# A 1 MB weight load dealt as 119 and 9 partitions, in a mixture-of-experts layer on one core

## The chip, the cores and the metric

The kernel runs on one core of a Trainium2 chip. Its time is that of the device, in microseconds, from the start to the end of one execution; of several executions the median counts. The core has TensorE (PE in the rows, with PEld for its weight loads), VectorE (DVE), ScalarE (ACT), GpSimd (POOL) and SyncE (SP), and 16 DMA engines that all its transfers share.

## The reference, cut to what matters

One decoder layer on 256 tokens of 1024 columns, in float32. First a mixing part (retention and block attention), then a mixture of 32 experts, of which each token takes four:

```
h2 = rms_norm(x, norm2_w)                       # 256 x 1024
logits = h2 @ w_router + b_router               # 32 experts
gate, chosen = softmax over the top 4 logits
for each expert e, for its tokens:
    u = h2[tokens] @ w1[e] + b1[e]              # 1024 -> 2048
    a = clamped_swiglu(u)                       # -> 1024
    x[tokens] += gate * (a @ w2[e] + b2[e])     # 1024 -> 1024
out = rms_norm(x, final_norm_w)
```

An expert has 8 MB of `w1` (the first layer) and 4 MB of `w2` (the second). All 32 are read once: 384 MB.

## The kernel before

The expert part takes 64 token slots per expert. The tokens of an expert are gathered by a matmul with a 0/1 matrix, turned, multiplied with `w1` (`up`, its matmuls at L1444), put through the SwiGLU, turned again, multiplied with `w2` (`down_part`, L1466), and added back by another 0/1 matmul (`combine`, L1415).

The weights stream through `ring`, an area of 24 slots of 1 MB, used as 12 pairs of 2 MB. A step of the loop over experts has six chunks of 2 MB: chunks 0 to 3 are the `w1` of expert j, chunks 4 and 5 the two halves of `w2` of expert j - 1. So step j does the up projection of expert j and the down projection of expert j - 1. Chunk `(j, k)` goes to pair `pair_of(j, k)`. Steps 6 to 17 of the source form the body of a loop that runs twice, in which `w1` chunks are loaded two at a time (4 MB, L430); the last steps stand behind it. Step 30 is written out as `LAST - 1`, step 31 as `LAST`, and step `E` = 32 holds only the last down projection.

SyncE issues every weight load, in the order of use, into one queue. Before each it waits until PE has used what stood in the pair (`chunk_used`). `load` (L432 to L445) picks the form: most chunks are one DMA of 128 partitions by 16 KB (L443 for `w1`, L445 for `w2`). The chunks in `END_HALVES`, the last ones of the kernel, are two DMAs of 128 partitions by 8 KB (L440, L441), and the very last chunk is three DMAs (L437), so that PE can begin with a part. The DMAs of a pair count up its semaphore `pair_full[d]` by 16.

PE's `down` (L1471) waits for `pair_full` of its chunk, then does 16 matmuls over the whole chunk: columns 0 to 2047 of the pair (slots `2d`) with the activations `c` = 0, 1, and columns 2048 to 4095 with `c` = 2, 3.

Bias rows are loaded once, near 111 us, by three DMAs of 32 partitions by 4 KB (L456, L457). `final_norm_w` is loaded last (L536).

Of the kernel before, what the change touches and what calls it, by code (L numbers as in the profile page):

```python
# [23 lines left out]
P = 128  # L24
SEQ = 256
T = SEQ // P
D = 1024
# [21 lines left out]
W1_CHUNKS = C // 2  # L49
# [7 lines left out]
LAST = E - 1  # L57
BIAS_STEP, RESID_STEP = 4, 5
LAST_PARTS = [(0, 2), (2, 3), (3, 4)]
END_HALVES = [(LAST, W1_CHUNKS), (LAST, W1_CHUNKS + 1), (E, 0)]  # L60
assert PEEL + ITERS * UNROLL + 2 == E and TURNS * PAIRS == UNROLL * STEP_CHUNKS
SENTINEL = 3.0e38
# [33 lines left out]
def local_expert(i, j):  # L96

    return i * UNROLL + j
# [7 lines left out]
def down_chunk(j, k):  # L106

    return k if j == E else k - W1_CHUNKS

def place_in_stream(j, k):

    return k if j == 0 else j * STEP_CHUNKS - W2_CHUNKS + k

def pair_of(j, k):

    return place_in_stream(j, k) % PAIRS
# [7 lines left out]
def pair_count(r, i, j, k):  # L126

    g = place_in_stream(j, k)
    per_round = len(range(g % PAIRS, ROUND_CHUNKS - 1, PAIRS))
    if g % PAIRS in {pair_of(j, k) for j in (PEEL, PEEL + 1) for k in range(1, W1_CHUNKS, 2)}:  # L130
        in_loop = ITERS * TURNS
        return 16 * (r * (per_round - in_loop) + (g // PAIRS + 1) - (in_loop if j >= PEEL + UNROLL else 0))
    return 16 * (r * per_round + i * TURNS + (g // PAIRS + 1))

def layer_kernel(nc, x, norm1_w, w_in, ret_norm_w, w_out, norm2_w, w_router, b_router,
# [6 lines left out]
    w2_v = w2.rearrange("l e (q p s) n -> (l e) q p (s n)", p=P, s=4)  # L143

    ctx = ExitStack()
    with ctx:
# [3 lines left out]
        def sem(name):  # L150
            return ctx.enter_context(nc.semaphore(name))
# [4 lines left out]
        def bank(b, n=1):  # L156
            return PS[:, b * BANK:(b + n) * BANK]
# [103 lines left out]
        head_full = [sem(f"head_full{s}") for s in range(HEAD_CHUNKS)]  # L261
        last_in = [sem(f"last_in{k}") for k in range(len(LAST_PARTS))]
        half_in = [sem(f"half_in{k}") for k in range(len(END_HALVES))]
        pair_full = [sem(f"pair_full{d}") for d in range(PAIRS)]
        chunk_used = sem("chunk_used")
        early_used = sem("early_used")
        early_in = [sem(f"early_in{k}") for k in range(len(EARLY))]
# [126 lines left out]
        def _(sp):  # L394
# [14 lines left out]
            for j, pair in enumerate(WOUT_ORDER):  # L409
                s = WIN_CHUNKS + j  # L410
                dst = ring[:, s, :].rearrange("p (c n) -> p c n", c=2)
# [10 lines left out]
            def w1_half(e, k):  # L422

                return w1_v[e, k // 2, :, (k % 2) * 2 * SLOT_COLS:(k % 2 + 1) * 2 * SLOT_COLS]
# [7 lines left out]
            def load(r, i, j, k):  # L432
                e, d = local_expert(i, j), pair_of(j, k)
                dst = ring[:, 2 * d:2 * d + 2, :].rearrange("p a n -> p (a n)")
                if j == E and k == W2_CHUNKS - 1:
                    for part, (a, b) in enumerate(LAST_PARTS):
                        sp.dma_start(dst[:, a * D:b * D], w2_v[e - 1, k, :, a * D:b * D]).then_inc(last_in[part], 16)  # L437
                elif (j, k) in END_HALVES:
                    src = w2_v[e - 1, down_chunk(j, k), :, :]
                    sp.dma_start(dst[:, 0:2 * D], src[:, 0:2 * D]).then_inc(half_in[END_HALVES.index((j, k))], 16)  # L440
                    sp.dma_start(dst[:, 2 * D:], src[:, 2 * D:]).then_inc(pair_full[d], 16)  # L441
                elif j < E and k < W1_CHUNKS:
                    sp.dma_start(dst, w1_half(e, k)).then_inc(pair_full[d], 16)  # L443
                else:
                    sp.dma_start(dst, w2_v[e - 1, down_chunk(j, k), :, :]).then_inc(pair_full[d], 16)  # L445

            for g in FIRST_ORDER:
                if g == 10:
                    sp.wait_ge(decayed_ready, RET_HEADS)
                    sp.wait_ge(chunk_used, WIN_CHUNKS)  # L450
                elif g == 11:
                    sp.wait_ge(probT_ready, MOBA_HEADS)
                    sp.wait_ge(pv_done, 4)
                    sp.wait_ge(ret_done, RET_HEADS)
                    for v in range(2):
                        sp.dma_start(b1_sb[v * E:(v + 1) * E, :], b1[0, :, v * F:(v + 1) * F]).then_inc(late_in, 16)  # L456
                    sp.dma_start(b2_sb, b2[0, :, :]).then_inc(late_in, 16)  # L457
                    sp.wait_ge(gated, T)
                elif g == 8:
                    sp.wait_ge(retT_done, 2)  # L460
                elif g == 9:
                    sp.wait_ge(retT_done, 2)
                    sp.wait_ge(chunk_used, HEAD_CHUNKS - 2)
                else:
                    sp.wait_ge(chunk_used, min(2 * g + 2, HEAD_CHUNKS))
                if g == MOVED:
                    d = pair_of(0, g)
                    sp.dma_start(ring[:, 2 * d, :], w1_half(0, g)[:, 0:SLOT_COLS]).then_inc(pair_full[d], 16)
                    sp.dma_start(ring[:, 2 * d + 1, :], w2_v[1, 1, :, SLOT_COLS:]).then_inc(ahead_in, 16)
                elif g < W1_CHUNKS:  # L470
                    load(0, 0, 0, g)
                else:
                    load(0, 0, 1 + (g - W1_CHUNKS) // STEP_CHUNKS, (g - W1_CHUNKS) % STEP_CHUNKS)
# [619 lines left out]
        def _(pe):  # L1093
# [325 lines left out]
            def wait_early(r, g):  # L1419

                if isinstance(r, int) and g - PAIRS in EARLY:
                    pe.wait_ge(early_in[EARLY.index(g - PAIRS)], 16)
                    if g - PAIRS in QUARTERS:
                        pe.wait_ge(early_v0_in[QUARTERS.index(g - PAIRS)], 16)
# [35 lines left out]
            def down_part(j, k, c0, c1, aT_n, out):  # L1460

                d, h = pair_of(j, k), down_chunk(j, k)
                for c in range(c0, c1):
                    for half in range(2):
                        cols = (c % 2) * D + half * BANK
                        last = mm(out[64 * half:64 * half + 64, :], aT_n[:, c, 64 * h:64 * h + 64],  # L1466
                                  ring[:, 2 * d + c // 2, cols:cols + BANK],
                                  start=(h == 0 and c == 0), stop=(h == 1 and c == 3))
                return last

            def down(r, i, j, k):  # L1471

                pe.wait_ge(pair_full[pair_of(j, k)], pair_count(r, i, j, k))
                g = place_in_stream(j, k)
                wait_early(r, g)
                if isinstance(r, int) and g == AHEAD:
                    pe.wait_ge(ahead_in, 16)
                aT_n, out = (aT_last, bank(1)) if j == E else (aT, bank(5))
                down_part(j, k, 0, 4, aT_n, out).then_inc(chunk_used, 1)

            def down_first(r, j, k):

                pe.wait_ge(half_in[END_HALVES.index((j, k))], 16 * (r + 1))
                aT_n, out = (aT_last, bank(1)) if j == E else (aT, bank(5))
                down_part(j, k, 0, 2, aT_n, out)

            def down_rest(r, i, j, k):

                pe.wait_ge(pair_full[pair_of(j, k)], pair_count(r, i, j, k))
                aT_n, out = (aT_last, bank(1)) if j == E else (aT, bank(5))  # L1490
                down_part(j, k, 2, 4, aT_n, out).then_inc(chunk_used, 1)
# [21 lines left out]
            def end_step(r, i):  # L1513
# [5 lines left out]
                down_rest(r, i, E, 0)  # L1519
                for part, (c0, c1) in enumerate(LAST_PARTS):  # L1520
                    pe.wait_ge(last_in[part], 16 * (r + 1))
# [7 lines left out]
            def expert_pe(r, i, j):  # L1529
# [16 lines left out]
                if j > 0:  # L1546
                    pe.wait_ge(actT_ready, n)
                    for k in range(W1_CHUNKS, STEP_CHUNKS):
                        down(r, i, j, k)
# [96 lines left out]
```

## Time and profile before

| | |
|---|---|
| median of 3 runs | 1052.78 us (1052.59 to 1054.54) |
| the profiled execution | 1053.78 us |
| its span, first to last instruction | 1052.0 us |
| PE busy | 1028.2 us, 98% |
| VectorE, ScalarE busy | 221.5, 117.5 us |
| queue q1, share of the 16 DMA engines | 96.3% |
| moved | 424.62 MB, mean 404 GB/s |

A share of 1 in a column "DMA share" means that all 16 DMA engines are busy in that stretch; packets that overlap at their ends can bring it a little over 1. PE's matmuls are pipelined and their ends modelled, so that small waits don't show as idle time. "Issue to landing" of a DMA runs from its issue on SyncE to the last count of its semaphore, and includes the time in the queue behind earlier ones.

### The profile page before, as it was taken

How to read it: one execution, taken by the hardware profiler on the slowest of the kernel's cores; microseconds unless marked ns; L12 is line 12 of the kernel's file. 1: busy time of each engine (PE TensorE's matmuls, PEld its weight loads, DVE VectorE, ACT ScalarE, POOL GpSimd, SP SyncE). 2: the span in 40 equal slices, each digit the busy share in tenths (PEclk: the TensorE clock that was granted, in tenths of full speed). 3: DMA queues.
4: the chain of work that ended last, by engine and by line, in shares of the span. 5: the costliest groups of instructions: out<-in, count | busy, mean ns of one | idle time of the engine just before them, and what ended most of it. 6: DMA issues, size and time to landing. Idle time of an engine off the chain costs nothing.

```text
span 1052.0 us, 11246 instructions
## 1 busy us (share of the span) xinstructions
PE 1028.2 (98%) x4918; PEld 415.7 (40%) x4918; DVE 221.5 (21%) x585; ACT 117.5 (11%) x223; POOL 0.2 (0%) x4
## 2 busy tenths in 40 slices
PE   9999999999999999999999999999999999998996
PEld 8888543333333333333333333333333333323332
DVE  2173442111111111111111111111111111111111
ACT  2131130000000000000000000000000000000002
POOL 0000000000000000000000000000000000000000
PEclk9999999999999999999999999999999999999999
DMA  9982999999999999999999999999999999999995
GB/s 320 369 363 80 351 371 386 410 429 434 420 424 400 437 427 430 434 428 429 427 425 431 434 429 430 430 430 433 424 427 428 433 432 427 433 428 426 428 422 224
DMA packets 39126, 424.62 MB, mean 404 GB/s; under 512 B 3512, under 2 KB 16320, under 8 KB 19744
## 3 DMA queue, kind: packets, MB, share of 16 engines
q1 hardware_dynamic: 38768, 423.51, 96.3%
q8 instruction: 41, 0.67, 0.3%
q10 hardware_dynamic: 304, 0.33, 0.1%
q14 instruction: 13, 0.11, 0.0%
HBM read 422.78 MB, written 1.05 MB: 403 GB/s over the span
## 4 chain that ended last, share of the span: by engine, by line
PE 92%; DMA 5%; another core or an unknown queue 1%; DVE 1%; issue 0%; ACT 0%; SPq 0%; DVEq 0%; ACTq 0%
PE PS L1444 41%; PE PS L1466 20%; PE PS L1122 8%; PE PS L1415 5%; DMA ring<-in_w 5%; PE PS L1398 5%; PE PS L1303 3%; PE PS L1259 3%; PE PS L1497 2%; PE PS L1407 2%; PE PS L1390 1%; DMA ring<-in_w_in 1%; PE PS L1571 0%; PE PS L1585 0%; PE PS L1192 0%
## 5 line engine op out<-in xcount | busy, mean ns | idle before, releaser
L1444 PE MATMUL PS<-ring,work 128*64 128x512 f32 x2040 | 448.7, 596 | 12.0 <-DMA ring<-in_w 10.7
L1444 PEld LDWEIGHTS PS<-ring,work 128*64 128x64 f32 x2040 | 143.9, 137 | 291.9 <-issue 273.4
L1466 PE MATMUL PS<-ring,work 128*64 128x512 f32 x1024 | 227.4, 595 | 0.1
L1466 PEld LDWEIGHTS PS<-ring,work 128*64 128x64 f32 x1024 | 70.6, 137 | 153.8 <-issue 151.1
L1015 DVE TENSOR_SCALAR work<-PS 128x512 f32<-128x512 f32 x32 | 22.1, 692 | 401.1 <-PE PS L1444 401.1
L1122 PE MATMUL PS<-ring 128*128 128x256 f32 x384 | 85.4, 380 | 0.3 <-DMA ring<-in_w_in 0.3
L644 ACT ACTIVATE work<-work 128x512 f32<-128x512 f32 x32 | 20.2, 630 | 535.3 <-DVE work L1015 535.3
L1122 PEld LDWEIGHTS PS<-ring 128*128 128x128 f32 x384 | 72.0, 190 | 10.8 <-DMA ring<-in_w_in 0.7
L983 DVE TENSOR_TENSOR work<-PS,n2w 128x512 f32<-128x512 f32 x30 | 20.8, 692 | 228.3 <-PE PS L1407 228.3
L1415 PE MATMUL PS<-late,work 64*128 64x512 f32 x248 | 61.9, 616 | 0.0
L1398 PE MATMUL PS<-resid,work 128*64 128x512 f32 x248 | 58.5, 592 | 0.0
L661 ACT ACTIVATE late<-PS 128x512 f32<-128x512 f32 x30 | 17.9, 597 | 209.6 <-PE PS L1466 209.6
L1303 PE MATMUL PS<-work 32*64 32x512 f32 x256 | 34.8, 613 | 0.0
L1398 PEld LDWEIGHTS PS<-resid,work 128*64 128x64 f32 x248 | 17.8, 137 | 35.4 <-issue 35.4
L991 DVE COPY work<-PS 128x256 f32<-128x256 f32 x31 | 13.2, 425 | 85.9 <-PE PS L1390 85.9
L1415 PEld LDWEIGHTS PS<-late,work 64*128 64x128 f32 x248 | 21.3, 186 | 19.4 <-issue 15.8
L1407 PEld LDWEIGHTS PS<-cst,work 128*128 128x128 f32 x124 | 17.3, 209 | 25.4 <-issue 24.3
L1497 PE MATMUL PS<-cst,work 128*128 128x128 f32 x128 | 23.9, 309 | 0.5
L1407 PE MATMUL PS<-cst,work 128*128 128x128 f32 x124 | 23.2, 310 | 0.1
L1019 DVE SCALAR_TENSOR_TENSOR work<-work 128x512 f32<-128x512 f32 x32 | 22.2, 692 | 3.3
L1022 DVE TENSOR_TENSOR work<-work 128x512 f32<-128x512 f32 x32 | 22.1, 692 | 1.1
L664 ACT ACTIVATE work<-PS 128x512 f32<-128x512 f32 x31 | 18.5, 597 | 30.8 <-PE PS L1497 30.8
(173 smaller groups left out, 370.2 us busy)
## 6 DMA issues: line engine op xcount, KB each, us to landing
ring<-in_w SPq DMA_DIRECT2D x48, 4096.0 KB, 34.9
ring<-in_w SPq DMA_DIRECT2D x85, 2048.0 KB, 27.1
ring<-in_w SPq DMA_DIRECT2D x18, 1024.0 KB, 9.7
ring<-in_w_in SPq DMA_DIRECT2D x11, 1024.0 KB, 11.9
ring<-in_w_out SPq DMA_DIRECT2D x4, 1024.0 KB, 12.1
ring<-in_w SPq DMA_DIRECT2D x6, 512.0 KB, 6.9
ring<-in_w_in SPq DMA_DIRECT2D x2, 512.0 KB, 6.3
ring<-in_consts SPq DMA_DIRECT2D x1, 800.0 KB, 11.2
```

The source lines that it names most:

```text
L1015: nc.vector.tensor_scalar(g_sb, bank(0), LIMIT, None, ALU.min).then_inc(gate_ready, 1)
L1019: nc.vector.scalar_tensor_tensor(a_sb, a_sb, 1.0, g_sb, ALU.add, ALU.mult).then_inc(glin_ready, 1)
L1022: nc.vector.tensor_tensor(a_sb, a_sb, s_sb, ALU.mult).then_inc(act_ready, 1)
L1122: last = mm(bank(4 + j % 2)[:, t * WIN_COLS:(t + 1) * WIN_COLS], hT[:, t, c, :], w[:, c, :], start=(c == 0), stop=(c == C - 1))
L1259: return mm(bank(2 + 4 * t + j), mixT(c)[:, t * P:(t + 1) * P], w[:, c % 2, j * BANK:(j + 1) * BANK], start=(c == 4), stop=(c == 3))
L1303: last = mm(bank(v)[64 * half:64 * half + 64, :], sel[v * E:(v + 1) * E, :], b1_sb[v * E:(v + 1) * E, half * BANK:(half + 1) * BANK], star ...
L1398: last = mm(bank(4)[64 * half:64 * half + 64, :], pick[:, t, :], resid[:, t, half_cols(half)], start=(t == 0), stop=(t == T - 1))
L1407: last = nc.tensor.transpose(bank(4)[:, c * P:(c + 1) * P], gx_v[:, c, :], ident)
L1415: last = mm(bank(2 + 4 * t + half), put[rows, t * P:(t + 1) * P], y[rows, :], start=start, stop=False, skip_group_check=True)
L1444: last = mm(bank(v)[64 * half:64 * half + 64, :], gh[:, c, :], w[:, v * F + half * BANK:v * F + (half + 1) * BANK], start=False, stop=(c = ...
L1466: last = mm(out[64 * half:64 * half + 64, :], aT_n[:, c, 64 * h:64 * h + 64], ring[:, 2 * d + c // 2, cols:cols + BANK], start=(h == 0 and ...
L1497: last = nc.tensor.transpose(out[:, c * P:(c + 1) * P], a_v[:, c, :], ident)
```

## The change

Chunk 4 of step 30, the first half of expert 29's second layer, is loaded as three DMAs instead of one: columns 0 to 2047 in two DMAs, of the rows 0 to 118 and 119 to 127, and columns 2048 to 4095 in one of 128 rows. The first two count up a semaphore of their own, `split_in`, for which PE's `down` waits beside `pair_full`.

```diff
+SPLIT, SPLIT_ROWS = (LAST - 1, W1_CHUNKS), 119
...
+        split_in = sem("split_in")
...
                     sp.dma_start(dst[:, 0:2 * D], src[:, 0:2 * D]).then_inc(half_in[END_HALVES.index((j, k))], 16)
                     sp.dma_start(dst[:, 2 * D:], src[:, 2 * D:]).then_inc(pair_full[d], 16)
+                elif (j, k) == SPLIT:
+                    src = w2_v[e - 1, down_chunk(j, k), :, :]
+                    for rows in (slice(0, SPLIT_ROWS), slice(SPLIT_ROWS, P)):
+                        sp.dma_start(dst[rows, 0:2 * D], src[rows, 0:2 * D]).then_inc(split_in, 16)
+                    sp.dma_start(dst[:, 2 * D:], src[:, 2 * D:]).then_inc(pair_full[d], 16)
                 elif j < E and k < W1_CHUNKS:
...
                 if isinstance(r, int) and g == AHEAD:
                     pe.wait_ge(ahead_in, 16)
+                if (j, k) == SPLIT:
+                    pe.wait_ge(split_in, 32 * (r + 1))
```

## Rows read from the trace of the kernel before

**Rows 1.** The page: busy time by engine, and the DMA queues.
```profile
PE 1028.2 (98%) x4918; PEld 415.7 (40%) x4918; DVE 221.5 (21%) x585; ACT 117.5 (11%) x223; POOL 0.2 (0%) x4
q1 hardware_dynamic: 38768, 423.51, 96.3%
```

**Rows 2.** Stages; columns: stretch, length, busy by engine, PE's clock, DMA share, GB/s.
```profile
300.00:500.00 200.00, 199.88 (x943) 69.66 (x940) 33.88 (x77) 16.95 (x28) 0.00 (x0) 1.00 1.00 426
700.00:900.00 200.00, 194.60 (x922) 66.76 (x918) 33.91 (x77) 16.95 (x28) 0.00 (x0) 1.00 1.01 430
```

**Rows 3.** The chain that ended last, steady stage: start, length, what (one of three).
```profile
899.71 1.64 another core or an unknown queue
```

**Rows 4.** The same chain, the last experts.
```profile
958.39 2.49 another core or an unknown queue
...
960.93 8.78 PE PS L1444 x32
...
983.19 13.88 PE PS L1444 x64
...
999.81 7.02 PE PS L1466 x32
...
1024.44 3.43 PE PS L1466 x16
...
1028.77 3.58 PE PS L1466 x16
1032.36 0.13 issue
...
1035.49 5.49 PE PS L1466 x24
```

**Rows 5.** SyncE's DMA issues in order of time: start, length, line, count.
```profile
111.14 0.80 SPq L456 DMA_DIRECT2D work<-in_b  x2
...
944.04 6.46 SPq L445 DMA_DIRECT2D ring<-in_w  x2
...
1002.24 16.14 SPq L437 DMA_DIRECT2D ring<-in_w  x3
```

**Rows 6.** One line's DMAs: first that of L445 at 944.04 alone.
```profile
DMA to landing us min/median/max: 51.5/51.5/51.5
L440 SPq DMA_DIRECT2D ring<-in_w x3: 4241/4245/4599, 976.2 to 993.7; - x3
DMA to landing us min/median/max: 38.7/42.3/46.3
L437 SPq DMA_DIRECT2D ring<-in_w x3: 1137/2712/12207, 1002.2 to 1015.7; - x3
DMA to landing us min/median/max: 24.1/35.0/35.1
```

**Rows 7.** The end of the stream, in stretches; columns as in rows 2.
```profile
1033.00:1034.00 1.00, 1.00 (x8) 0.29 (x4) 0.00 (x0) 0.98 (x2) 0.00 (x0) 1.00 1.05 414
1034.00:1035.00 1.00, 1.00 (x6) 0.30 (x4) 0.00 (x0) 0.50 (x2) 0.00 (x0) 1.00 0.71 295
1035.00:1037.00 2.00, 2.00 (x12) 0.48 (x8) 0.00 (x0) 0.00 (x0) 0.00 (x0) 1.00 0.55 227
...
1039.00:1040.00 1.00, 1.00 (x8) 0.32 (x6) 0.00 (x0) 0.00 (x0) 0.00 (x0) 1.00 0.31 119
1040.00:1041.00 1.00, 1.00 (x8) 0.19 (x4) 0.00 (x0) 0.00 (x0) 0.00 (x0) 1.00 0.10 41
```

**Rows 8.** Stretches around the three loads of 32 partitions.
```profile
113.00:115.00 2.00, 2.00 (x6) 0.95 (x5) 1.62 (x14) 0.21 (x1) 0.00 (x0) 1.00 1.01 434
118.00:118.50 0.50, 0.50 (x2) 0.19 (x1) 0.47 (x2) 0.00 (x0) 0.00 (x0) 1.00 0.99 221
118.50:119.50 1.00, 1.00 (x4) 0.40 (x3) 0.54 (x1) 0.00 (x0) 0.00 (x0) 1.00 1.06 279
```

**Rows 9.** PE's clock after its long stop.
```profile
961.80:965.10 3.30, 3.30 (x10) 0.98 (x8) 0.00 (x0) 0.00 (x0) 0.00 (x0) 0.50 0.99 422
```

## The prediction before the run

> **What bounds the kernel now.** I read the page first, then the stages, then the tail piece by piece. The page says two things at once: PE is busy for 98% of the span, and the queue of the loads, q1, keeps the 16 DMA engines busy for 96.3% of it [rows 1]. The stages tell them apart. From 300 to 900 us the DMA share is 1.00 to 1.01 at 426 to 430 GB/s, and nothing else is full [rows 2]. An expert is 12 MB of weights, and the chain repeats the same pattern: PE works through 32 + 32 + 8 + 8 + 32 + ... matmuls and then stands for 1.6 us (three times from 870 to 931, one row shown) [rows 3]. So up to the last three experts the weight stream is the bound, and PE has some 1.6 us to spare per expert.
>
> At the end this turns. The last long stop is 2.49 us at 958.39. From 983.19 on the chain is PE alone [rows 4]: two up projections of 13.88 us (the second, at 1010.56, is like the one shown), without a stop, and down projections behind them. PE and the stream are then nearly equal. How near is read from pieces of the same kind. Sixteen down matmuls take 3.43 us at 1024.44 but 3.58 us at 1028.77; 0.13 us is "issue"; and the last 24 take 5.49 us, where 24 at the rate of the undisturbed 32 in 7.02 us would take 5.27. That is 0.15 + 0.13 + 0.22 = 0.5 us of waiting for weights in the last 58 us, and no more. The last megabyte, in three parts, is issued from 1002.2 to 1015.7, and its parts land 24.1 to 35.1 us later, the very last at 1015.7 + 24.1 = 1039.8 [rows 5, 6], and PE ends the down projection that needs it at 1040.98. So in the tail a landing that is earlier can give at most 0.5 us, and one that is later is paid in full.
>
> **Where the changed DMA sits.** It is the first half of the 2 MB load that SP issues at 944.04; that lands 51.5 us later, at 995.5 [rows 5, 6]. PE wants it at 999.81 [rows 4], so 4.3 us of cover. It isn't the chunk itself that matters then, but what the 16 engines have behind it: 2 MB + 4 x 2 MB + the 1 MB and 0.5 MB pieces, all queued on the same engines without a gap up to 1039.8.
>
> **What it adds.** (a) One DMA becomes three: two more issues at 0.33 us on SP. SP issues the later ones 24 to 50 us ahead of their landing [rows 6], and where its issue takes 4 to 16 us [rows 5] it waits for room in queues that are full, so that this is hidden; were it not, it would be under 1 us. Each more DMA has a completion entry of its own on each engine: the 1 MB pieces of L440 and L441 land from 976.2 + 46.3 = 1022.5 to 993.7 + 38.7 = 1032.4, four pieces in 9.9 us or 2.48 us each [rows 6], while 1.05 MB at the 430 GB/s of the larger loads [rows 2] are 2.44 us; the 0.04 us are for the entry, twice 0.08. (b) PE waits for one more semaphore before the first half of a down projection. Behind it stand on PE the 32 down matmuls, the turning of rows and activations, the combine and the last up projection, and VectorE and ScalarE wait for those; with 4.3 us of cover it costs nothing unless the piece is over 4.3 us late.
>
> **(c) How the rows are dealt.** This is the term that decides. 128 rows are 8 rows for each of 16 engines. 119 = 7 x 17 can't be dealt evenly to 16; even shares exist on seven engines (or one) only, and 9 rows are one each on nine. I take it that the shares are even: 17 rows on each of seven engines, then one more row on these and on two others. The trace of before has no load with such a number, so the bounds are uneven dealing (7 or 8 rows each, no effect) and this.
> The Trainium skill ("DMA: Bandwidth & Descriptors", section "Why a DMA increments its semaphore by 16 and not by 1") states that the engine count is the largest number up to 16 that divides the slowest dimension, and that the lowest-numbered engines are taken; by that it is seven and nine. No row of this profile shows it.
>
> An 8 KB row at 430 GB/s / 16 = 26.9 GB/s is 0.305 us. The seven have 18 rows to do instead of 8: 10 x 0.305 = +3.05 us on them, and the other nine 7 or 8 rows less, -2.1 to -2.4 us.
>
> **(d) Are the seven the ones that are ahead?** The 16 engines do not end together. The DMA share is 1.05 at 1033, 0.71 in 1034 to 1035, then 0.55, then 0.31 in 1039 to 1040 and 0.10 in the last microsecond before 1041 [rows 7]. 9 of 16 is 0.56: seven engines run dry at about 1034.3 (0.71 is 0.56 + 0.34 of the other 0.44), all of them before 1035, and nine work on until 1039.7 on average (1039 + 0.41/0.56) and 1041.0 at the latest. So seven are 6.7 us ahead on average and at least 6.0. Every load waits for its slowest engine. If the seven that get more are those seven, +3.05 us is inside their lead, and the nine end earlier. If they are others, all +3.05 us is paid. The counts agree and no row gives the engines' numbers; I take "the same seven" at 4 to 1.
>
> **(e) Do they write at full speed?** In before each engine always takes the same rows of a 128-row load. There is one place with other shapes: three bias loads of 32 rows each, issued from 111.14 on [rows 5]. While they pass, the engines are as busy as ever (share 0.99 to 1.06) and move 221 and 279 GB/s, against 434 ahead of them [rows 8]. Engines that write rows other than those of the usual deal slow one another, down to 221/434 = 0.51 of the rate. So for the 18 rows the bounds are 18 x 0.305 = 5.5 us (full speed) and 18 x 0.61 = 11.0 us (half). Against 8 x 0.305 = 2.44 us in before that is +3.05 or +8.5 us. For the nine others, half speed on what they meet takes back the 2.1 to 2.4 us. I take half speed for the most unlucky of the seven, because rows 8 are the nearest thing here, and the load ends with its slowest engine.
> The Trainium skill ("SBUF — State Buffer", section "Door 1: The DMA port swizzle") gives a port to each group of 8 partitions and 27.2 GB/s to a port; with that, seven engines that reach all 119 partitions write through the ports of the nine as well. The trace agrees as far as rows 8 go; in those rows half of the ports would carry it all.
>
> **The sum.** Seven leading engines, the slowest at half rate: +8.5 - 6.0 (least lead) = +2.5, and entries 0.1, and some 0.2 because a PE that now stops does not stop at the best places: +2.8 us. Nothing in the tail hides it: PE's own slack is there already used up, the last landing moves, and the ends of the down projection, of the last combine and of the norm move with it. The profiled execution took 1053.78 us for a span of 1052.0, which would become 1056.6 and 1054.8; it was 1.0 above the median of 1052.78, so the median becomes 1055.6.
>
> **The rivals.**
> R1, not slower: the seven are the leaders and write at full speed. Then the nine decide, end 2.1 us earlier, and PE is the bound: of 2.1 us only the 0.5 us of waiting can be had, less 0.1: 1052.4. For it: the lead of 6.0 to 6.7 is twice the 3.05 us. Against it: rows 8. It holds as long as the seven lose less than 6.0 us, that is while their rate in the 18 rows stays over 0.65 of full.
> R2: the seven are not the leaders. At full speed +3.1, 1055.9; at half speed +8.5 and up to 1061.3. For it: nothing ties the numbers of the engines to their lead. Against: seven and nine on both sides.
> R3: the change doesn't do that. Rows are dealt as evenly as can be on 16 engines, nothing but 0.1 us of entries: 1052.9.
> R4, on top of the forecast or of R2: PE's clock. PE stood for 2.49 us from 958.39 on [rows 4], and in the stretch behind that the granted clock was 0.50, which is 1.2 GHz [rows 9]; the 32 matmuls in it took 8.78 instead of 7.09 us: 1.7 us. Stops of 1.6 us, one per expert, did not do it [rows 3]. If the new waits come in one piece like that one, the end is at 1057.3.
>
> **How the numbers follow.** Forecast (leaders, about half rate, 1.5 to 5 us lost) 0.38, with R4's share in it; R1 0.25; R2 0.15; R3 0.12; the seven only a little slower than their lead allows, 0 to 1.5 us lost, 0.10. A measurement tells about 0.2%, 2.1 us. Slower by more: most of the forecast (0.34), all of R2 (0.15) and a little of the rest with R4 (0.06): 0.55. Within: 0.43. Faster by more: only were PE not the bound, 0.02. The range of 8 in 10 goes from R1 (1052.1) to half of R2 (1059.0).
>
> **What would show it.** If the even deal is right: a DMA share that differs in the tail from 0.56 for 4 to 5 us. In the forecast all 16 engines end within some 2 us of one another, the share stays near 1 up to some 1038, and the last landing is at about 1042.6; the chain has stops for weights of 2 to 3 us in all after 1002. In R1 the share stays near 1 up to 1037 and then falls at once, and the pieces of the last down projections are down to 3.43 us for 16. In R2 the engines that are last stand alone: a share of 0.44 or less for up to 9 us. In R3 rows 7 come back as they are. The stream itself must slow just once, around 985 to 996, if writing is what costs: GB/s under 400 at a share of 1. If GB/s stays at 430 there, step (e) is wrong; if the last landing is over 1043.5, the leads were read wrongly.

## The result: 13 us slower, and the trace after

Timed side by side on one chip, the changed kernel takes 1067.93 us (median of 4 runs, 1066.18 to 1070.96), the kernel before 1053.58 (4 runs, 1052.59 to 1054.54). The ratio is 1.0127, 95% interval 1.0104 to 1.0151: about +13.4 us (the medians by themselves are 14.35 apart). I had forecast 1055.6, which is +2.8, with a range up to 1059.0. The profiled execution took 1066.18 us for a span of 1064.4.

Page of the kernel after, totals by engine (busy us, share, instructions). PE is busy for 5.8 us more than before with the same work:

```profile
span 1064.4 us, 11248 instructions
PE 1034.0 (97%) x4918; PEld 416.8 (39%) x4918; DVE 221.4 (21%) x585; ACT 117.6 (11%) x223; POOL 0.2 (0%) x4
```

Where it goes is seen in the stages. Kernel after, busy time by stretch; the last three columns are PE's granted clock, DMA share and GB/s, as in [rows 2]:

```profile
980.00:984.00 4.00, 4.00 (x22) 1.51 (x22) 1.47 (x6) 0.00 (x0) 0.00 (x0) 1.00 1.07 412
984.00:988.00 4.00, 4.00 (x22) 1.35 (x20) 0.00 (x0) 0.00 (x0) 0.00 (x0) 1.00 1.01 246
988.00:992.00 4.00, 2.94 (x14) 0.72 (x10) 0.00 (x0) 0.00 (x0) 0.00 (x0) 1.00 0.95 205
992.00:996.00 4.00, 0.62 (x2) 0.30 (x4) 0.00 (x0) 0.00 (x0) 0.00 (x0) 0.66 1.05 225
996.00:1000.00 4.00, 4.00 (x12) 1.19 (x10) 0.00 (x0) 0.00 (x0) 0.00 (x0) 0.50 1.02 227
1000.00:1004.00 4.00, 4.00 (x22) 0.91 (x18) 2.45 (x4) 1.05 (x2) 0.00 (x0) 0.99 1.01 246
...
1006.00:1010.00 4.00, 1.87 (x6) 0.72 (x8) 0.00 (x0) 0.00 (x0) 0.00 (x0) 0.62 1.02 436
```

For 20 us the 16 engines are as busy as ever and move about half. It isn't only the changed half: in 20 us they would have moved 8.6 MB, and in these 20 us they moved some 4.6. The loads ahead of the half and behind it slow down with it. To size it, one stretch that holds all of it, of the kernel before and then of the kernel after:

```profile
976.00:1024.00 48.00, 47.96 (x230) 17.05 (x227) 6.47 (x15) 3.62 (x6) 0.00 (x0) 1.00 1.01 426
```

```profile
976.00:1024.00 48.00, 39.49 (x164) 13.84 (x162) 6.46 (x15) 3.62 (x6) 0.00 (x0) 0.86 1.01 339
```

The share is the same 1.01. I call **stream lost** what is missing in the bytes, in us: 48 x (1 - 339/426) = 9.8 us.

The landings, lines of DMA issues of the kernel after (first the last `w1` chunk of step 30, which the change doesn't touch; then the third DMA of the split chunk; then the very last parts), and the counterpart of the first in the kernel before:

```profile
L450 SPq DMA_DIRECT2D ring<-in_w x1: 328/328/328, 937.4 to 937.4; - x1
DMA to landing us min/median/max: 57.9/57.9/57.9
...
L448 SPq DMA_DIRECT2D ring<-in_w x1: 3597/3597/3597, 957.4 to 957.4; - x1
DMA to landing us min/median/max: 50.6/50.6/50.6
...
L439 SPq DMA_DIRECT2D ring<-in_w x3: 3933/4240/4243, 1017.2 to 1025.8; - x3
DMA to landing us min/median/max: 26.5/29.6/32.6
```

```profile
L443 SPq DMA_DIRECT2D ring<-in_w x1: 328/328/328, 937.7 to 937.7; - x1
DMA to landing us min/median/max: 52.9/52.9/52.9
```

The `w1` chunk ahead of the split lands at 937.4 + 57.9 = 995.3 instead of 990.6 (+4.7). The split chunk lands at 957.4 + 50.6 = 1008.0 instead of 995.5 [rows 6] (+12.5). The very last part lands at 1025.8 + 26.5 = 1052.3 instead of 1039.8 (+12.5), and PE ends the last down projection at 1053.53 instead of 1040.98. So nothing is added or given back after 1008: the place costs 12.5 us and the tail hands it on. (This execution was 0.8 us ahead of the one of before until then: the second `w1` chunk of step 30 landed at 980.03 instead of 980.81. Counted from there the loss is 13.3, which agrees with the 13.4 of the ratio.)

PE's queue of the kernel after, start and length, with the idle time ahead in brackets, shows the two stops:

```profile
995.38 5.98 PE L1451 MATMUL PS<-ring,work 128*64 128x512 f32 x16 [4.44 <-DMA ring<-in_w]
...
1008.13 4.54 PE L1473 MATMUL PS<-ring,work 128*64 128x512 f32 x10 [4.04 <-DMA ring<-in_w]
```

The end of the stream, kernel after, columns as above; it answers to [rows 7]:

```profile
1036.00:1040.00 4.00, 4.00 (x21) 1.37 (x18) 2.67 (x4) 0.63 (x1) 0.00 (x0) 1.00 1.01 417
1040.00:1042.00 2.00, 2.00 (x14) 0.85 (x12) 0.42 (x1) 0.60 (x1) 0.00 (x0) 1.00 0.96 391
1042.00:1044.00 2.00, 1.92 (x12) 0.48 (x8) 0.00 (x0) 0.00 (x0) 0.00 (x0) 1.00 0.79 320
1044.00:1046.00 2.00, 1.40 (x9) 0.43 (x7) 0.00 (x0) 1.45 (x2) 0.00 (x0) 1.00 0.82 330
1046.00:1050.00 4.00, 4.00 (x20) 1.06 (x18) 0.00 (x0) 0.64 (x2) 0.00 (x0) 1.00 0.28 116
1050.00:1053.00 3.00, 3.00 (x16) 0.93 (x16) 0.00 (x0) 0.00 (x0) 0.00 (x0) 1.00 0.11 44
```

Before, nine engines worked together almost to the end. Now 0.28 of 16 is 4 to 5 engines and 0.11 is two: the engines end farther apart. Capacity left unused until the last landing: 2 x 0.04 + 2 x 0.21 + 2 x 0.18 + 4 x 0.72 + 2.3 x 0.89 = 5.8 us, against 0.29 + 4 x 0.45 + 0.8 x 0.69 = 2.6 before [rows 7]. These 3.2 us and the 9.8 of the stream make 13.0; the landing moved by 12.5.

**Which engines had the 119 rows.** The semaphores' counts in the trace of after give the ends of each engine's part (us). First the `w1` chunk ahead, then both pieces of the split half, then the third DMA:

```
w1 ahead   983.7 983.7 983.7 983.8 984.0 984.1 984.9 | 986.8 | 991.7 991.8 992.3 992.5 993.0 993.1 994.3 995.3
119 + 9    (944.2 957.6) 984.5 984.8 993.4 993.4 994.0 994.3 994.4 994.8 994.9 995.5 998.3 998.9 1004.3 1004.6 1005.4 1005.8
third DMA  988.2 988.5 988.8 996.6 996.7 997.1 997.3 997.7 997.8 998.7 998.7 999.3 1000.0 1003.2 1007.0 1008.0
```

The two in brackets come right after the issues. Behind them are 16 = 7 + 9 counts, one for each engine that did a part.
The Trainium skill ("DMA: Bandwidth & Descriptors", section "Why a DMA increments its semaphore by 16 and not by 1") says that the issuer counts at once for the engines that a DMA doesn't use, and gives seven and nine; this line agrees.

In the first line seven engines lead by some 8 us (in the second `w1` chunk of step 30, where nothing is slowed yet, by 4 to 6: 973.9 to 974.6 against 978.3 to 980.0). Had they had the 17 rows, no count of the split could stand at 984.5 and 984.8, and no third-DMA part at 988.2 to 988.8. Three leaders had none of the 17. The rest follows from 8 rows at some 0.6 us behind each end. Six ends of the third DMA, 996.6 to 997.8, stand 4.7 to 4.9 us behind the first six laggards of the first line (991.7 to 993.1), so that these had none either. So the seven that did were four leaders, the one in the middle and two laggards. Four leaders in the seven, three outside: a lead has nothing to do with the dealing.

The last two ends of each line are those two laggards: from 994.3 and 995.3 to 1004.6 and 1005.8, 18 rows in 10.3 and 10.5 us. That is 0.57 to 0.58 us a row, near the half rate that I had taken (0.61).

### The profile page after: what moved, and what is told of

Read it like the earlier page. It is cut to its first block, busy times and chain, and to the rows that moved or that the text cites. A ratio compares the mean times of both kernels' runs of the same rounds, so it can differ in the third digit from the quotient of the medians.

```text
span 1064.4 us, 11248 instructions
## 1 busy us (share of the span) xinstructions
PE 1034.0 (97%) x4918; PEld 416.8 (39%) x4918; DVE 221.4 (21%) x585; ACT 117.6 (11%) x223; POOL 0.2 (0%) x4
## 3 DMA queue, kind: packets, MB, share of 16 engines
HBM read 422.78 MB, written 1.05 MB: 398 GB/s over the span
## 4 chain that ended last, share of the span: by engine, by line
PE 83%; DMA 13%; SPq 2%; DVE 1%; another core or an unknown queue 1%; issue 0%; ACT 0%; DVEq 0%; ACTq 0%
PE PS L1451 36%; PE PS L1473 17%; DMA ring<-in_w 13%; PE PS L1129 8%; PE PS L1422 5%; PE PS L1405 4%; PE PS L1266 3%; PE PS L1310 2%; PE PS L1506 2%; PE PS L1414 2%; SPq L443 2%; PE PS L1397 1%; DMA ring<-in_w_in 1%; PE PS L1580 0%; PE PS L1594 0%
## 5 line engine op out<-in xcount | busy, mean ns | idle before, releaser
L1451 PE MATMUL PS<-ring,work 128*64 128x512 f32 x2040 | 451.3, 599 | 14.4 <-DMA ring<-in_w 13.3
L998 DVE COPY work<-PS 128x256 f32<-128x256 f32 x31 | 13.2, 425 | 86.0 <-PE PS L1397 86.0
```

What stands on the lines that cost most here:

```text
L1451: last = mm(bank(v)[64 * half:64 * half + 64, :], gh[:, c, :], w[:, v * F + half * BANK:v * F + (half + 1) * BANK], start=False, stop=(c = ...
```

## The experiments

Each edit is shown against the changed kernel; all times are against the kernel before on the same chip. The column "us" is the ratio less 1, times the median of before; the medians themselves differ from that by up to 1.3 us. "Lost" is the stream lost as above, from the one row 976 to 1024 of each trace (before: 426 GB/s). "Ahead" and "split" are by how much the `w1` chunk ahead and the split chunk land later than before. They are counted from the landing of the second `w1` chunk of step 30, from which before needs 9.78 and 14.69 us.

| cut of the half | GB/s | lost | ahead | split | ratio (95%) | us |
|---|---|---|---|---|---|---|
| by columns, 1904 and 144 | 424 | 0.2 | 0.0 | 0.1 | 1.0008 (0.9986 to 1.003) | +0.8 |
| own rows only | 425 | 0.1 | 0.0 | 0.1 | 1.0004 (0.9983 to 1.0025) | +0.4 |
| other rows only | 379 | 5.3 | 3.8 | 6.1 | 1.0041 (1.0025 to 1.0057) | +4.3 |
| 112 and 16, of 1024 columns | 401 | 2.8 | 2.8 | 3.5 | 1.0014 (0.9997 to 1.0031) | +1.5 |
| 64 and 64 | 371 | 6.2 | 4.9 | 6.7 | 1.0057 (1.0033 to 1.0081) | +6.0 |
| 112 and 16 | 365 | 6.9 | 5.6 | 7.5 | 1.0069 (1.0052 to 1.0087) | +7.3 |
| 120 and 8 | 373 | 6.0 | 4.4 | 7.1 | 1.0072 (1.0054 to 1.0091) | +7.6 |
| 117 and 11, first run | 366 | 6.8 | 4.8 | 7.5 | 1.0053 (1.0036 to 1.007) | +5.6 |
| 117 and 11, second run | 366 | 6.8 | 4.8 | 7.6 | 1.0072 (1.004 to 1.0104) | +7.6 |
| 115 and 13 | 354 | 8.1 | 6.2 | 9.0 | 1.0092 (1.0068 to 1.0116) | +9.7 |
| 114 and 14 | 352 | 8.3 | 6.0 | 13.2 | 1.0118 (1.0086 to 1.015) | +12.5 |
| 119 and 9 (the change) | 339 | 9.8 | 5.5 | 13.3 | 1.0127 (1.0104 to 1.0151) | +13.4 |
| 119 and 9, again | 336 | 10.1 | 6.2 | 13.8 | 1.0136 (1.0108 to 1.0165) | +14.4 |

### Is it the rows, or one DMA more?

The half in two DMAs of all 128 rows, with nearly the same bytes in each.

```diff
-                    for rows in (slice(0, SPLIT_ROWS), slice(SPLIT_ROWS, P)):
-                        sp.dma_start(dst[rows, 0:2 * D], src[rows, 0:2 * D]).then_inc(split_in, 16)
+                    for cols in (slice(0, 1904), slice(1904, 2 * D)):
+                        sp.dma_start(dst[:, cols], src[:, cols]).then_inc(split_in, 16)
```

> The half is cut by columns instead of rows: three DMAs as in the changed kernel, all of 128 partitions (1904, 144 and 2048 columns). Theory M (rows that reach partitions other than those of the usual deal slow the whole stream) and theory I (ten more rows on each of seven engines): both expect the time of before, within 0.5 us, and a stream at 420 to 430 GB/s all through 984 to 1004 us. Theory N (it is the number of DMAs, their entries, or the wait added on PE): expects a good part of the 12 us of the change here too.

1.0008: nothing. Busy time by stretch of this kernel, columns as above:

```profile
984.00:988.00 4.00, 4.00 (x22) 1.31 (x20) 0.00 (x0) 0.00 (x0) 0.00 (x0) 1.00 1.01 418
...
992.00:996.00 4.00, 4.00 (x22) 1.29 (x18) 0.94 (x2) 0.21 (x1) 0.00 (x0) 1.00 1.04 440
```

The three issues, the wait and the entries cost nothing that can be told: the interval of the times reaches from -1.5 to +3.2 us, but the split chunk lands only 0.1 us later. All that follows is the cut by rows.

### Is it the uneven deal?

112 and 16 rows are even on 16 engines, 120 and 8 on 15 and 8.

```diff
-SPLIT, SPLIT_ROWS = (LAST - 1, W1_CHUNKS), 119
+SPLIT, SPLIT_ROWS = (LAST - 1, W1_CHUNKS), 112
```

> The rows are cut as 112 and 16: both numbers divide evenly over 16 engines (7 and 1 rows each), so no engine gets more than before, but nearly every engine writes other partitions than in a DMA of 128. Theory M: most of the loss of the change stays, plus 6 to 12 us over before, and the stream runs at 200 to 300 GB/s at a DMA share near 1 for 10 to 20 us. Theory I: the time of before, within 0.5 us, since no engine has more to do.

> Rows cut as 120 and 8: 15 engines with 8 rows, then 8 engines with one more; the most loaded engine has 9 rows instead of 8, 0.3 us more. Theory I: plus 0.3 us or less. Theory M: plus 6 to 12 us, as with 112 and 16.

+7.3 and +7.6 us: more than half of the loss is there with 8 rows, or at most 9, for each engine. Kernel with 112 and 16, busy time by stretch:

```profile
984.00:988.00 4.00, 4.00 (x22) 1.41 (x21) 1.48 (x6) 0.00 (x0) 0.00 (x0) 1.00 1.07 227
988.00:992.00 4.00, 4.00 (x22) 1.43 (x20) 0.00 (x0) 0.00 (x0) 0.00 (x0) 1.00 0.94 287
992.00:996.00 4.00, 3.03 (x16) 0.72 (x10) 0.00 (x0) 0.00 (x0) 0.00 (x0) 1.00 1.04 233
996.00:1000.00 4.00, 2.72 (x8) 0.88 (x10) 0.00 (x0) 0.00 (x0) 0.00 (x0) 0.65 1.02 264
1000.00:1004.00 4.00, 4.00 (x20) 1.12 (x16) 1.29 (x2) 0.63 (x1) 0.00 (x0) 0.92 0.95 391
```

The same full share with 227 to 287 GB/s, for 16 us instead of 20. The uneven deal is what the change has on top of this, some 6 to 7 us.

### The same engines, bytes and count, on own or on other rows

Eight DMAs of 8 rows each, one row for each of eight engines. One kernel loads rows 0 to 63 so, in sets that leave each row to the engine that has it in a 128-row load; the other loads rows 64 to 127 with the same engines. The other 64 rows of the half aren't loaded in either, so that both leave part of the weights out.

```diff
-                    for rows in (slice(0, SPLIT_ROWS), slice(SPLIT_ROWS, P)):
+                    for first in (0, 1, 2, 3, 32, 33, 34, 35):
+                        rows = slice(0 + first, 0 + first + 29, 4)      # the other kernel: 64 + first
                         sp.dma_start(dst[rows, 0:2 * D], src[rows, 0:2 * D]).then_inc(split_in, 16)
...
-                    pe.wait_ge(split_in, 32 * (r + 1))
+                    pe.wait_ge(split_in, 128 * (r + 1))
```

> Instead of the two row pieces, eight DMAs of 8 rows by 8 KB: rows 0 to 63 in steps of four (0, 4, ... 28; 1, 5, ... 29; and so on; then 32 to 63). Rows 64 to 127 of the half are not loaded, so the output is not the reference's. An even deal is one row for each of eight engines. If in a DMA of 128 rows the first eight engines have rows 4e to 4e+3 and 32+4e to 35+4e, every row here is written by the engine that usually writes it. Theory M (it counts whether rows go to their usual engine): time of before or up to 1.3 us less, since eight engines move 0.5 MB less and the last may be among them; the stream never under 380 GB/s. Theory S (it is small or unevenly dealt DMAs that cost): plus 5 us or more, here and with rows 64 to 127 alike.

> The same eight DMAs, on rows 64 to 127; rows 0 to 63 of the half are not loaded, so the output is not the reference's. Same count, bytes and engines as its twin, but every row is one that another engine usually writes. Theory M: 0.5 MB on foreign rows, half of the 1 MB that cost 7.3 us with 112 and 16: plus 2.5 to 5 us over the twin, with the stream at 200 to 300 GB/s for 5 to 10 us. Theory S: within 0.5 us of the twin.

1.0004 and 1.0041; the intervals (to 1.0025, from 1.0025) only touch, and the median of the second is 5.6 us over that of the first. The traces leave less doubt. Own rows:

```profile
988.00:992.00 4.00, 4.00 (x22) 1.43 (x20) 0.00 (x0) 0.00 (x0) 0.00 (x0) 1.00 1.01 424
992.00:996.00 4.00, 4.00 (x22) 1.29 (x19) 0.92 (x2) 0.20 (x1) 0.00 (x0) 1.00 1.05 446
996.00:1000.00 4.00, 4.00 (x24) 1.08 (x22) 1.75 (x3) 1.03 (x2) 0.00 (x0) 1.00 0.98 418
```

Other rows (this execution was some 5 us late before step 30 had begun, so that its stretch stands later):

```profile
988.00:992.00 4.00, 4.00 (x22) 1.38 (x20) 0.00 (x0) 0.00 (x0) 0.00 (x0) 1.00 1.03 272
992.00:996.00 4.00, 4.00 (x20) 1.15 (x16) 0.00 (x0) 0.00 (x0) 0.00 (x0) 1.00 0.98 248
996.00:1000.00 4.00, 0.80 (x4) 0.29 (x4) 0.00 (x0) 0.00 (x0) 0.00 (x0) 0.81 1.05 295
```

This is the pair that settles the mechanism. Small DMAs, partial row counts and eight of 16 engines cost nothing; rows that another engine writes in the loads around cost the whole stream 5.3 us for 0.5 MB.
The Trainium skill ("DMA: Bandwidth & Descriptors", section "The descriptor swizzle") says which: engine e of 0 to 7 writes rows 4e to 4e + 3 and 32 + 4e to 32 + 4e + 3, and 8 to 15 the same from row 64 on. The two kernels were cut by that, and they agree.

The packets in the traces show the same one by one. With own rows the 16 KB packets of the ordinary loads take 611 to 627 ns each from 984 to 994 us, and the 8 KB packets 309 to 326. With other rows, from 990 to 994, the ordinary ones take 1039 to 1251 ns and the 8 KB ones 615 on average. In the changed kernel, from 988 to 996, the averages are 1206 and 612. Both sides of a collision run at half rate. What the pair doesn't tell is whether they collide where the rows are read or where they are written, since a row has the same number in `w2` and in the ring.

### How many engines share, and how few

64 and 64 rows, and 127 and 1.

```diff
-SPLIT, SPLIT_ROWS = (LAST - 1, W1_CHUNKS), 119
+SPLIT, SPLIT_ROWS = (LAST - 1, W1_CHUNKS), 64       # the other kernel: 127
```

 If it is the number of engines on the same rows' places that counts, two engines then share each of eight places in either DMA: plus 2.4 us at least (1 MB at half rate), and up to 7. Theory I (uneven deal alone): nothing.

> Rows cut as 127 and 1: an even deal exists on one engine only, which then has 128 rows instead of 8, 120 x 0.305 = 36.6 us more. Theory I: plus 36.6 us less the lead of that engine (0 to 6.8 us), so 30 to 37 us over before; the other 15 stay at their full rate, the stream at about 15/16 of 430 GB/s until they run dry. Theory M: one engine that visits all partitions also slows itself, row by row to half rate or less where it meets another: plus 40 to 75 us. If the deal is not even (uneven on 16 engines), plus nothing by I.

64 and 64 cost 6.0 us (3.5 to 8.5), over the 3 to 4.5 of a cost by rows and inside the 2.4 to 7 of its rival; the interval excludes neither. But the stream lost is 6.2 us against 6.9 with 112 and 16, so that the cost hardly fell. 127 and 1 cost 48.9 us (ratio 1.0463, 1.0434 to 1.0493), inside the 40 to 75 of theory M and over the 30 to 37 of theory I: one engine has all 128 rows. SyncE's queue and the busy time by stretch of that kernel:

```profile
947.02 55.38 SPq L447 DMA_DIRECT2D ring<-in_w  x2
1002.44 1.15 SPq L448 DMA_DIRECT2D ring<-in_w  x1
```

```profile
984.00:988.00 4.00, 4.00 (x22) 1.39 (x20) 1.48 (x6) 0.00 (x0) 0.00 (x0) 1.00 0.84 356
988.00:992.00 4.00, 4.00 (x22) 1.31 (x20) 0.00 (x0) 0.00 (x0) 0.00 (x0) 1.00 0.46 195
992.00:996.00 4.00, 4.00 (x20) 1.29 (x18) 0.00 (x0) 0.00 (x0) 0.00 (x0) 1.00 0.08 31
996.00:1000.00 4.00, 4.00 (x22) 1.29 (x18) 1.18 (x2) 0.46 (x1) 0.00 (x0) 1.00 0.06 27
```

Two things are read here. SyncE's two issues take 55 us, during which it can't issue the next load, and the other 15 engines run dry. And the one engine, alone, moves 27 GB/s, the full rate of one engine (430/16 = 26.9), though most of its rows are other engines' rows. So a foreign row isn't slow in itself. The packets bear this out. This engine's 8 KB packets take 309 to 318 ns from 986.4 to 992.8 and from 994.2 to 1004. From 1008 to 1034, when the others are at work again, they average 570 and reach 709, and some 16 KB packets of the others take over 1200 instead of 611. In the first of these stretches some half of the engines were still busy (share 0.46) and nothing slowed. So it isn't traffic as such that slows a foreign row and what it meets; that it is the row's usual writer at work at the same moment fits this and the pair above, but no count or packet carries an engine's number.

### How much, and where

112 and 16 with half the bytes (columns 0 to 1023; the rest of the half in one DMA of 128 rows; `down` waits for 48 counts), and both cuts at step 5 instead of step 30, where the engines are some 3 us apart instead of 6 to 7 (ends of one chunk by the counts: 249.4 to 252.7 in the kernel with 119 and 9 at step 5, 973.9 to 980.0 in the changed one).

```diff
-                        sp.dma_start(dst[rows, 0:2 * D], src[rows, 0:2 * D]).then_inc(split_in, 16)
+                        sp.dma_start(dst[rows, 0:D], src[rows, 0:D]).then_inc(split_in, 16)
+                    sp.dma_start(dst[:, D:2 * D], src[:, D:2 * D]).then_inc(split_in, 16)
...
-SPLIT, SPLIT_ROWS = (LAST - 1, W1_CHUNKS), 119
+SPLIT, SPLIT_ROWS = (5, W1_CHUNKS), 119              # the other kernel: 112
```

> 112 and 16 rows, but only of columns 0 to 1023 (0.5 MB); columns 1024 to 2047 as one DMA of 128 rows. Theory M with cost by bytes on foreign rows: half of the 7.3 us of the full half, plus 2.5 to 5 us. Were the cost one per DMA (a switch between two ways of dealing), it would stay at plus 6.5 to 8 us.

> The 119 and 9 rows in step 5 instead of step 30, chunk 4, near 220 us. There the stream bounds, PE stops 1.6 us per expert and waits for every landing, and the loads are issued only some 12 to 15 us ahead. Theory M with uneven deal: what the stream loses is never given back, plus 9 to 14 us, as late in the kernel; the stream at 200 to 300 GB/s for up to 20 us near 220. If the loss hangs on the deep queue of the late stage (50 us of loads waiting), it is under half here: plus 2 to 6 us.

> 112 and 16 rows in step 5 instead of step 30. 119 and 9 there cost 6.2 us, half of the late place. If the late place is dearer because the engines are there 6 to 7 us apart (foreign rows of the leading ones slow the others in the load before, and the other way round later) and early only 2 to 3 us apart, then both parts shrink: plus 1 to 3 us. If only the uneven part shrinks and foreign rows cost the same everywhere: plus 6 to 7 us, no less than 119 and 9 there.

Half the bytes lose 2.8 us of stream, two fifths of the 6.9, and +1.5 us in the time (-0.3 to +3.3), under the 2.5 to 5 expected and not told from nothing; in the trace the split chunk lands 3.5 us late. A fixed cost per DMA (6.5 to 8 us) is excluded. The cost isn't proportional to the bytes either: 0.5 MB lost 2.8 us of stream here and 5.3 in the kernel with other rows. At step 5, 119 and 9 cost 6.2 us (1.0059, 1.0041 to 1.0078) instead of 13.4, between the two forecasts and near the one for a cost that hangs on the late stage. 112 and 16 cost 1.4 us (1.0013, 1.0 to 1.0026) instead of 7.3: both parts shrink. Stretch 240 to 280 of the kernel before, of 119 and 9, and of 112 and 16:

```profile
240.00:280.00 40.00, 39.97 (x185) 14.61 (x182) 5.54 (x12) 3.62 (x6) 0.00 (x0) 1.00 1.01 430
```

```profile
240.00:280.00 40.00, 39.96 (x184) 14.43 (x178) 5.53 (x12) 3.62 (x6) 0.00 (x0) 1.00 1.01 361
```

```profile
240.00:280.00 40.00, 39.96 (x185) 14.59 (x182) 5.54 (x12) 3.62 (x6) 0.00 (x0) 1.00 1.02 388
```

Lost by the same formula: 40 x (1 - 361/430) = 6.4 us and 3.9 us, against 9.8 and 6.9 late. So the same cut slows the stream itself less there. That fits a collision that lasts longer when the engines come to the piece at different times, but the early place differs in more than that (fewer loads are queued ahead of it), and no run separates the two. Nor did PE wait there, as I had expected: it is busy for 39.96 of the 40 us, in the kernel before too. The 6.2 us come later, where the stream is the bound.

### What the uneven deal adds

If the engine with the most rows sets the end, the loss follows its rows. The number in `SPLIT_ROWS` is all that changes: 117, 119 again, 114 = 6 x 19 and 115 = 5 x 23.

> Rows cut as 117 and 11: nine engines with 13 rows, then eleven with one more, so the most loaded has 14 rows instead of 8, 6 more. Foreign rows at half rate are some 0.57 us each (10 more of them made 119 and 9 land 5.7 us later than 120 and 8). Foreign rows and uneven deal together: 7.3 + 5 x 0.57 = plus 10 us over before (9 to 11.5). If only the foreign rows count: plus 7.3, as 112 and 16. If the extra of 119 and 9 came from the seven alone (fewer engines, other rows): anything near 7 or near 13.

> 117 and 11 once more, beside the others of its kind on one chip: at most 14 rows on an engine. Theory U (foreign rows cost some 7 us, and each row over the 14 or so that the engines' different leads and the mutual slowing hide costs 0.57 to 0.6 us, half rate): plus 6 to 8 us over before. Theory V (the uneven deal costs nothing, 119 and 9 was dear for another reason): 6 to 8 us too.

> The changed kernel itself again: at most 18 rows. Theory U: plus 9 to 14 us; it should stand 4 x 0.57 = 2 us or more over 117 and 11. Theory V: within 1 us of 117 and 11 on the same chip.

> 114 = 6 x 19: 19 rows on each of six engines, then one more on 14, so at most 20 rows. Theory U: some 1.1 us over 119 and 9. Theory V: as 117 and 11, 6 to 8 us.

> 115 = 5 x 23: 23 rows on each of five engines, then one more, at most 24. Theory U: 6 x 0.57 = 3.4 us over 119 and 9, 15 to 17 us over before; if fewer visiting engines slow each other less, nearer to full rate, 6 x 0.305 = 1.8 us over it. Theory V: as 117 and 11.

Measured: +5.6 and +7.6, +14.4, +12.5, +9.7. Taken by the most loaded engine's rows this order makes no sense, and none of the theories above gave it. The counts of the semaphores do explain it. Their number behind the issues is 24 for 117 and 11 (13 + 11), 20 for 114 and 14 (6 + 14), 18 for 115 and 13 (5 + 13), 23 for 120 and 8 (15 + 8) and 2 for 127 and 1. So 117 rows are 9 each on thirteen engines, with the second piece 10 on one; a reckoning with 14 on nine engines has the factor the wrong way round. And the engine that ends the half is followed from its end of the chunk ahead:

```
rows  pieces      ends chunk ahead   ends half   us a row
 8    112 + 16    997.2 (last)       1001.8      0.57
 9    120 + 8     994.6 (last)       1000.0      0.60
10    117 + 11    997.8 (last)       1003.3      0.55
18    119 + 9     995.3 (last)       1005.8      0.58
20    114 + 14    994.3 (last but 1) 1005.8      0.57
24    115 + 13    988.6 (8th of 16)  1003.5      0.62
```

Every cut in this table has nearly the same price per row. What differs is who pays it. With 119 and 9 both laggards are among the seven. With 114 and 14 a single engine ends late (third DMA 1008.0, the next at 1002.3), so one laggard is among the six, and with 115 and 13 none is among the five: in 5.5 us (998.0 to 1003.5) a laggard can't do 24 rows even at full speed. The 24 rows then start on an engine that was 9 us ahead. Counts carry no engine's number, so each start is a choice: the last end of the chunk ahead in the first four lines, and in the last two lines the one that gives the common price (for 114 and 14 the last, 995.9, would give 0.50). The last two lines are fitted, then, and not measured. With that said, the lead does shelter extra rows, as (d) had it, only not on these engines.

No run pointed to a version that beats the kernel before; the best of them equal it.

## Why the prediction was wrong

**What bounds the kernel**: held for the tail. "Nothing else is full" was a misreading: [rows 2] have PE at 199.88 of 200 us from 300 to 500, and it is at 49.86 of 50 still from 750 to 800 and at 46.73 from 800 to 850. PE starts to wait for the stream only there. A landing that is later in the tail is paid in full: +12.5 us at the split, at the last landing and (12.55) at PE's last down projection.

**(a), issues and entries**: held as far as can be told, 1.0008 with three DMAs by columns.

**(b), the wait**: 4.3 us of cover were there, and the piece came 12.5 late. What I had not counted at all is the load ahead of the split, late by 4.7 us, for which PE stood 4.44 us first. I had followed the change only from its own DMA on. A leading engine is at the split while the others still load the chunk ahead, and slows them there.

**(c), seven and nine**: held, by the counts.

**(d), "the same seven", at 4 to 1**: false. Three of the leaders had no part of the 17 rows and two laggards had. That both counts are seven was no evidence that they count the same engines. The -6.0 in the sum is therefore wrong as a whole: the slowest of the seven had no lead at all. Against the even cut this is 5.7 us of the loss, 18 rows instead of 8 on a laggard, at 0.57. The lead itself was sized nearly right: in the kernel before, the counts of the last chunk stand at 1034.5 to 1035.8 for seven engines and reach 1041.0 for the others, 5.2 to 6.5 us (I took 6.0 as the least).

**(e), the price of the other rows**: this is the other step that failed, and the one with the mechanism wrong. The half rate was right for the engine that it was applied to (0.57 us a row). It is wrong as a sum over that engine alone. With "for the nine others, half speed on what they meet takes back the 2.1 to 2.4 us" I closed the account; in fact everything that passes meanwhile goes at about half, on all 16 engines, 9.8 us of stream. [rows 8] could have shown it: 221 GB/s at full share was the rate of the whole stream, and in the trace the 16 KB packets of the other loads take 811 to 1221 ns there (117.5 to 119.5 us) instead of 611, as the bias rows' own packets take about twice their 159.

In place of +8.5 - 6.0 + 0.3 the terms are, from the landings: +5.5 for the chunk ahead, which foreign rows slow before the laggards come to the split at all; and 18 rows x 0.58 - 8 x 0.305 = +8.0 for the laggard (7.8 measured). Together 13.5 for 13.3. The even cut pays 5.6 and 1.9. Of the 10.7 us between this sum and the forecast's 2.8, the lead that wasn't there makes 6.0 and the chunk ahead, which I had at nothing, 5.5; the 8.5 and the 0.3 were 0.8 too high together.

**The rivals.** R1's 0.5 us came in no run. R2 was right on (d) and right in its +8.5 for an engine that isn't ahead (8.0 here), but like the forecast it leaves out the chunk ahead, so that its upper end of 1061.3 is still too low. R3's figure, nothing but the entries, is what the cut by columns does; its condition, an even deal of 119 rows, is false by the counts. R4's clock came (0.50 in 996 to 1000, 0.62 after 1006) and added nothing: PE waits again at 1008.13, and it ends 1.20 us behind the last landing in both kernels.

Of the signs that I had named, GB/s under 400 at a share of 1 came, and the last landing stood over 1043.5, which I had said would mean leads wrongly read. The tail neither ended together (forecast) nor fell at once (R1). R2's sign is the one that came: the last engines stand alone, at a share of 0.28 and 0.11 for 7 us.

**Shown:** the loss comes with the cut by rows, not with the count of DMAs; rows of other engines cause it, with engines, count and bytes equal; it takes other engines at work at the same time, and their packets slow down as well; it slows the whole stream, the chunk ahead included; the uneven deal adds 0.55 to 0.6 us a row where a laggard has them. **Argued only:** why the same cut is cheaper early; that it takes the row's usual writer at work, and not just any engine; whether reading or writing collides; and which engine had the 20 and the 24 rows.

## What to carry to other kernels

In a stream of loads that keeps all engines busy, give every DMA all 128 partitions and cut it by columns, which was free here. A cut by rows that hands rows to engines other than their usual ones brings the whole stream down to between half and two thirds of its rate for as long as it lasts (7.3 us for 1 MB late in this kernel, 1.4 us early), and a row count whose even shares fit on few engines adds to that (13.4 us for 119, 49 for 127). When a short stretch of a profile shows a full DMA share and half the GB/s, charge that to all traffic in it, ahead of the odd load and behind it, not to the odd load's own rows. A lead of some engines is no slack to spend unless the profile tells which engines they are.

## What the runs showed of the hardware

- One engine with most of its rows foreign to it, and no other traffic, ran at 27 GB/s, its full rate; with traffic the 16 moved 205 to 246 GB/s at a share of 0.95 to 1.05. Busy share alone can't tell the two apart.
- One engine with a long queue is enough to hold SyncE: its issues took 55.38 us, up to 1002.4, behind the 127 rows of one engine, while the other 15 had ended their last part by 994.2.
- Where foreign rows meet the ordinary loads, both kinds of packet take twice as long: 16 KB 1206 ns instead of 616, 8 KB 612 instead of 313 (changed kernel, 988 to 996; the 313 from the kernel with own rows).
- Once spread, the engines stay so: in the changed kernel the counts of a later 128-row load run from 1030.5 (three engines) over 1034.7 to 1038.1 (eleven) to 1041.5 and 1042.5 (the two laggards that had 17 rows).
- PE's clock was 0.50 after a stop of 4.44 us; the 16 up matmuls at 995.38 took 5.98 us, 374 ns each, where 64 take 13.88 us [rows 4] at the full clock, 217 ns.
